# Compressed keys and values one job later, selection rounds after the gate's turned part

## What is computed

```
h   = rms_norm(x) * (1 + scale) + shift            # scale, shift, gate = silu(c) @ w_ada + b_ada
f   = h @ w_in                                     # columns shared out among both mixers
ck  = silu(flat(cmp_k rows + pe) @ w1[0]) @ w2[0]  # compressed keys,   31 per prompt head, 15 per sample
cv  = silu(flat(cmp_v rows + pe) @ w1[1]) @ w2[1]  # compressed values
o_n = g0*attend(q, ck, cv) + g1*attend(selected blocks) + g2*attend(window)
o_d = attend over the top-k keys by the indexer's score   (k = 128 for the prompt, 65 for samples)
y   = x + gate * ((sig(m_n) * up(o_n*silu(z_n)) + sig(m_d) * up(o_d*silu(z_d))) @ w_out)
```

## Time and profile before

| | |
|---|---|
| median of 3 runs (lowest, highest) | 618.58 us (617.23, 623.91) |
| the profiled execution: time, span | 616.9 us, 615.1 us |
| mean granted clock of TensorE | 0.993 |
| PE busy | 585.8 us, 95% of the span |
| DVE busy | 337.8 us, 55% |
| ACT busy | 247.6 us, 40% |
| POOL busy | 151.4 us, 25% |
| DMA | 68.37 MB, mean 111 GB/s |

### The profile page before, as it was taken

How to read it: one execution, slowest core, us unless ns; L and a number is a source line. 1 busy time by engine, 2 the same in 40 slices (tenths; PEclk the granted TensorE clock), 3 DMA queues, 4 the chain that set the end, 5 groups by cost and what they waited for, 6 DMA issues and landing times.

```text
span 615.1 us, 12161 instructions
## 1 busy us (share of the span) xinstructions
PE 585.8 (95%) x4630; PEld 481.0 (78%) x4630; DVE 337.8 (55%) x847; ACT 247.6 (40%) x549; POOL 151.4 (25%) x196
## 2 busy tenths in 40 slices
PE   4999999998999999989999999999999999999995
PEld 1487776765776887766766769999999999998784
DVE  0454025968978556878766654442322633227873
ACT  6232245143131345656567545343222232223443
POOL 1226350360350445643644430000000000000130
PEclk9899999999899999999999999999999999999999
DMA  9991731421452264001301207229332242434003
GB/s 305 385 343 26 289 128 39 143 67 52 131 156 73 71 174 139 2 1 44 95 3 52 87 4 189 84 69 267 119 69 76 87 113 69 100 108 137 1 30 117
DMA packets 52426, 68.37 MB, mean 111 GB/s; under 512 B 5089, under 2 KB 34969, under 8 KB 52208
## 3 DMA queue, kind: packets, MB, share of 16 engines
q1 hardware_dynamic: 49744, 56.85, 30.4%
q10 hardware_dynamic: 1808, 6.31, 3.0%
q0 software_dynamic: 816, 4.43, 1.8%
HBM read 62.99 MB, written 6.66 MB: 113 GB/s over the span
## 4 chain that ended last, share of the span: by engine, by line
PE 85%; DVE 9%; issue 3%; ACT 2%; DMA 1%; POOL 0%; SPq 0%; DVEq 0%; ACTq 0%
PE psum L1162 29%; PE psum L935 8%; PE psum L937 7%; PE psum L936 7%; PE psum L1424 5%; PE psum L1392 4%; PE psum L1347 4%; PE psum L1262 3%; PE psum L1069 2%; PE psum L961 2%; DVE psum L2080 2%; PE psum L950 1%; DVE score L2004 1%; DVE top L2003 1%; DVE rT L1999 1%
## 5 line engine op out<-in xcount | busy, mean ns | idle before, releaser
L1552 ACT ACTIVATE w_hi<-stage 128x1024 fp32r<-128x1024 f32 (+2 forms) x56 | 56.1, 1002 | 159.8 <-PE psum L1162 94.0
L1894 DVE TENSOR_TENSOR w_lo<-stage,w_hi 128x1024 fp32r<-128x1024 f32 x34 | 41.7, 1225 | 111.2 <-ACT w_hi L1552 108.0
L1162 PE MATMUL psum<-hT_hi,w_hi 128*128 128x272 f32 x368 | 76.4, 289 | 0.6 <-DVE w_lo L1894 0.6
L1162 PE MATMUL psum<-hT_lo,w_hi 128*128 128x272 f32 x368 | 76.2, 288 | 0.0
L1162 PE MATMUL psum<-hT_hi,w_lo 128*128 128x272 f32 x368 | 75.9, 288 | 0.0
L845 POOL TENSOR_TENSOR w_lo<-stage,w_hi 128x1024 fp32r<-128x1024 f32 (+2 forms) x22 | 44.2, 2008 | 107.9 <-ACT w_hi L1552 107.9
L935 PE MATMUL psum<-w_hi,hT_hi 128*128 128x512 f32 (+3 forms) x192 | 69.4, 361 | 0.7 <-issue 0.5
L936 PE MATMUL psum<-w_hi,hT_lo 128*128 128x512 f32 (+3 forms) x192 | 66.8, 348 | 0.0
L937 PE MATMUL psum<-w_lo,hT_hi 128*128 128x512 f32 (+3 forms) x192 | 66.7, 347 | 0.0
L926 POOL TENSOR_TENSOR y<-y,final_g 128x512 f32<-128x512 f32 (+1 forms) x5 | 7.8, 1588 | 217.2 <-ACT merged L1782 217.2
L1162 PEld LDWEIGHTS psum<-hT_hi,w_hi 128*128 128x128 f32 x368 | 57.8, 188 | 1.1 <-DVE w_lo L1894 1.1
(11 more groups left out here) (346 smaller groups left out, 1122.0 us busy)
## 6 DMA issues: line engine op xcount, KB each, us to landing
stage<-in_w_in SPq DMA_DIRECT2D x14, 1024.0 KB, 5.3
stage<-in_w_ada SPq DMA_DIRECT2D x8, 1024.0 KB, 10.2
stage<-in_w_in SPq DMA_DIRECT2D x10, 512.0 KB, 5.3
staging<-in_x_prompt ACTq DMA_DIRECT2D x4, 512.0 KB, 5.7
cached<-in_cache_nsa_kv SPq DMA_DIRECT2D x32, 64.0 KB, 2.3
stage<-in_cache_nsa_kv SPq DMA_DIRECT2D x16, 128.0 KB, 2.1
stage<-in_state_nsa_win_kv SPq DMA_DIRECT2D x2, 1024.0 KB, 7.2
stage<-in_cache_dsa_kv SPq DMA_DIRECT2D x16, 128.0 KB, 2.1
```

The costliest lines, as they stand in the source:

```text
L1162: last = mm(out[:, h, :], left[w][:, k, P * x:P * x + P], halves(mov[m])[:, h, :], start=(k == 0 and w + m == 0), stop=(k == tiles - 1 and ...
L1552: last = A(dst, src, ACT.Copy)
L1894: last = tt(dst, src, hi.bitcast(F32), ALU.subtract)
```

## The change

In the list of small work "ck" moves from slot 3, between "mod" and "modT" of part (4, 1), to the front of slot 4. "cvp" and the two "cvs" move from slot 4, between "mod" and "modT" of part (5, 0), to the front of slot 5. In VectorE's list the eight rounds that stood ahead of the wait for "ck" now stand behind the copy of "modT" (4, 1); the four and four rounds that stood ahead of the wait for "cvp" now stand behind the copy of "modT" (5, 0). No instruction is added or taken away. The rounds are those of `take_top`: one `max` and one `match_replace`.

```diff
     queries(3, ROT, range(2, 4))
-    for kind, n, e in (("qs", ROT, "v"), ("hid", 0, "a"), ("mod", (4, 1), "a"), ("ck", 0, "v"), ("modT", (4, 1), "v")):
+    for kind, n, e in (("qs", ROT, "v"), ("hid", 0, "a"), ("mod", (4, 1), "a"), ("modT", (4, 1), "v")):
         add(3, kind, n, e)
+
+    add(4, "ck", 0, "v")
     queries(4, DSAQ, range(2))
...
-    for kind, n, e in (("qs", DSAQ, "v"), ("hid", 1, "a"), ("mod", (5, 0), "a"), ("cvp", 0, "v"), ("cvs", 0, "a"),
-                       ("cvs", 1, "v"), ("modT", (5, 0), "v")):
+    for kind, n, e in (("qs", DSAQ, "v"), ("hid", 1, "a"), ("mod", (5, 0), "a"), ("modT", (5, 0), "v")):
         add(4, kind, n, e)
-    for kind, n, e in (("mod", (5, 1), "a"), ("selx", 0, "a"), ("selx", 1, "a"), ("modT", (5, 1), "v"),
+    for kind, n, e in (("cvp", 0, "v"), ("cvs", 0, "a"), ("cvs", 1, "v"), ("mod", (5, 1), "a"), ("selx", 0, "a"), ("selx", 1, "a"), ("modT", (5, 1), "v"),
                        ("grow", 0, "v"), ("grow", 1, "v"), ("k", WIN, "a"), ("kn", WIN, "v")):
         add(5, kind, n, e)
...
                             tt(dst, dst, part_t, ALU.add).then_inc(*tell(aux_dve))
+                        if n == (4, 1):
+                            rounds(2, 8)
+                        elif n == (5, 0):
+                            rounds(2, 4)
+                            rounds(3, 4)
                         continue
-                    if kind == "ck":
-                        rounds(2, 8)
-                    elif kind == "cvp":
-                        rounds(2, 4)
-                        rounds(3, 4)
                     dve.wait_ge(aux_done, i + 1)
```

## The result

The changed kernel takes 636.86 us (median of 6 runs, 636.45 to 642.14) against 619.22 us for the kernel before (617.23 to 623.91): ratio 1.0292, 95% interval 1.0251 to 1.0333. It is slower, as forecast; the forecast was 638, range 631.5 to 643. The profiled execution took 636.45 us with a span of 634.6, 19.5 more than the span of before. Two spans of one execution each differ by other things too: in this one "hid" of slot 3 begins at 142.31 instead of 141.73, a difference that arises ahead of everything the change touches. So I count every milestone from the start of that "hid".

The account below looks back on a forecast made before the run. The prediction took PE to bound the kernel (85% of the chain of waits, busy 95% of the span). Its terms, 10.0 + 5.9 + 1.9 + 1.7 = 19.5 us onto 616.9, gave 636.4, as a median 638, range 631.5 to 643.

Parts of the forecast that it names:

- PE, slot 3: "ck" leaves slot 3, but "modT" still waits for ScalarE's copy of "mod": gain 0, PE's idle time 1.9 us.
- PE, slot 4: "ck" at the front is covered by the queries' wait: cost 0; "modT" at the end comes 1.0 us earlier.
- VectorE, job 3: Eight rounds behind "modT" delay job 3's reads, so PE ends job 4's first piece late: cost 10.0 us.
- VectorE, job 4: Four and four rounds behind "modT" delay job 4's reads beyond VectorE's idle time, PE waits: cost 5.9 us.
- PE, slot 5: "cvp" and "cvs" arrive ahead of "mod" with nothing to cover them: cost 1.9 us.
- clock: PE's granted clock falls after each long stall: cost 0 after the first, 1.7 us after the second.
- The 1.1 us that the prediction worked out for that case: Added to the sum if PE returned from both stalls at 1.2 GHz, the throttled clock.
- The 1.7 us added for the median: The kernel before's median, 618.58, lay 1.7 above its profiled execution; added to 636.4 to forecast the median, 638.
- C: Rival: only half the delay reaches PE because VectorE regains time; 13.1 us, so 631.7; chance 0.10.
- D: Rival: VectorE's room takes the moved rounds in full; -0.8 us, so 617.8, no difference; chance 0.04.
- A: Rival: the clock stays full after the stalls; 17.8 us more, so 636.4; chance 0.18.
- B: Rival: longer clock falls, "ck" uncovered, slot 4's turning and copying begun at half clock; 23.3 us, so 642; chance 0.15.

Follow-up runs that it names:

- e1: The changed kernel with VectorE's rounds of both slots put back under "hid", ahead of the wait for "modT": 623.31 us against 619.23, ratio 1.005.
- e4: The changed kernel with only the eight rounds of slot 3 put back under "hid": 629.1 us against 621.99, ratio 1.0121.
- e2: The kernel before with only VectorE's rounds moved behind the copy of "modT", no matmuls moved: 637.95 us against 619.23, ratio 1.0278.
- e3: The changed kernel with only the four and four rounds of slot 4 put back under "hid": 631.1 us against 619.22, ratio 1.0163.
- e8: The kernel before with four of slot 3's eight rounds moved behind the copy of "modT": 623.65 us against 621.99, ratio 1.004.
- e7: The changed kernel with unread extra matmuls, 24 ahead of job 4's sample tile and 30 ahead of job 5's: 640.24 us against 621.99, ratio 1.0302.
- e5: The kernel before with "ck" and "modT" (4, 1) at the head of slot 4, the eight rounds still under "hid": ratio 0.9955.
- e9: A repetition of e5, the same kernel measured again: ratio 0.9997.
- e6: As e5, but the four rounds of tile 2 ahead of job 3's reads are shared out to jobs 4 and 5: ratio 0.9994.
- e10: A repetition of e6, the same kernel measured again: ratio 0.9974.

## Why the prediction was right, point by point

- **PE, slot 3: 0.** Right. "modT" starts 12.18 us after "hid" in both traces, and the wait ahead of it is 1.90 us, as said.
- **PE, slot 4.** "ck" under cover: 0 forecast, 0.3 measured where nothing else delays the piece (e1 and e4, queries 37.48 after "hid" against 37.22). The prediction read the start of the last tile as 177.7. It is 177.89, so PE's path from VectorE's last read to the queries is 1.8 us (e1, e4) and not 1.5:

```profile
177.89 0.29 PE L935 MATMUL psum<-w_hi,hT_hi 128*128 128x280 f32 x1
```

The earlier "modT" shows: 0.87 us of wait, then its matmuls; it is spent in the second stall, as forecast, and comes out only where that stall is gone (e1, -0.6 at job 5's sample tile).
- **VectorE, job 3: 10.0 forecast, 9.0 measured.** The mechanism was right, the size off by one instruction. The mask that ends the samples' selection took 1.45 us in the kernel before and 0.30 here (last section), so 1.15 of the 10.0 came back. The first read started 24.84 us after the first late round instead of 25.98. e2 and e3 repeat the delay, 8.9 and 9.3, without and with the moved matmuls; e8 halves the rounds and gets 3.85. For the same reason the first stall is 6.24 us and not 7.3.
- **VectorE, job 4: 5.9 forecast, 6.3 measured** (15.28 - 9.01). e4 has it alone: 6.3.
- **PE, slot 5: 1.9, and clock: 1.7.** Together 3.6 measured (18.91 - 15.28). Of these 1.7 is the slower first piece of job 5 (5.94 us instead of 4.24), and 1.9 the moved steps. The clock falls inside each stall, at about 179.3 and 223.7, and is still at 0.50 when PE comes back:

```profile
179.00:180.00 1.00, 0.00 (x0) 0.65 0.75 203
...
181.00:182.00 1.00, 0.64 (x13) 0.50 0.00 0
...
223.00:224.00 1.00, 0.00 (x0) 0.84 0.00 0
```

The fall after the first stall cost nothing, as forecast (e7, 46.22 against 46.23). By the Trainium skill (TensorE: Matmul & The Clock Gate, "What's actually happening") the throttled state is the default: the trace agrees, the clock is 0.50 at both returns. The 1.1 us that the prediction worked out for that case did not come, since the reads set PE's pace there. The prediction's side remark of four matmuls a us in a fall against five to six behind it is a misreading: the count takes in every matmul that touches the window. From start to start they are 0.43 us apart in the fall at 156 (156.40, 156.82) and 0.23 behind it (159.23, 159.46).
- **Sum:** 9.0 + 6.3 + 1.9 + 1.7 = 18.9, forecast 19.5. The medians differ by 17.6. Some of the nearness is luck. The terms of the two VectorE stages were off by -1.0 and +0.4, and the profiled execution meets the 636.4 (636.45) only because its "hid" began 0.6 us later. The 1.7 us added for the median did not come either: the median of the changed kernel is 0.4 above its profiled execution.
- **Rivals.** C (half of the delay absorbed) and D (all of it) fell: e8 shows that even four rounds find no room, since the reads' pace passes the delay on tile by tile, and to the queries through GpSimd's adds. A (the clock stays full after the stalls) gave 636.4, which is nearer to the measured 636.86 than the forecast of 638, but its mechanism is refuted by the trace: the clock was 0.50 at both returns. B's longer falls with "ck" uncovered are not in this trace; e3 has such a one (clock 0.54 at 186 to 188, queries 9.3 us late instead of 9.0). The medians alone could not tell the forecast from A or B, since executions of the changed kernel go from 636.45 to 642.14. Of the chances, the forecast, A, B and C add up to 0.96, not 0.95.

## What to carry to other kernels

An instruction moved past a wait in an in-order list moves everything behind that wait too: ask first what the engine did while it waited. Here 21 us of selection were free only because they stood ahead of the wait, and moved behind it they cost about 15, three quarters of it. And judge the room ahead of a chain of per-tile reads at its last tile, not at its first: 2.8 us at the sample tile were 0.45 at the last one (read until 177.44, used from 177.89), and none at the queries, which start 0.15 us after the GpSimd add that follows the last read.

## What the runs showed of the hardware that I had not expected

**A VectorE instruction that takes 0.30 or 1.45 us.** The selection's mask (a TENSOR_SCALAR of 32 x 288) in the kernel before, and the GpSimd instruction that ran at the time:

```profile
164.56 1.45 DVE L2013 TENSOR_SCALAR score_sample<-score_sample 32x288 f32<-32x288 f32 x1
```

```profile
163.44 2.41 POOL L845 TENSOR_TENSOR w_lo<-stage,w_hi 128x1024 fp32r<-128x1024 f32 x1 [3.70 <-ACT w_hi L1552]
```

The mask ends at 166.01, GpSimd's instruction at 165.85. In e1 and e4, where it starts beside the same GpSimd work, it takes 1.44 and 1.40; in the other nine profiles, the changed kernel's among them, it starts outside it and takes 0.30. The two instructions of a round beside the same GpSimd work keep their 0.45 and 0.43 us. By the Trainium skill (SBUF — State Buffer, "Who interferes with whom") VectorE and GpSimd share a port pair, whoever is first holds it for its whole instruction, and a `tensor_scalar` is of the kind that can ask for it; the traces agree in that VectorE's instruction ends 0.16 us after GpSimd's; the ports themselves no run shows. I had priced 25.98 us of VectorE work as one block and not looked for such a row in it.

**The same kernel with and without a fall of the clock.** e5 and e9 are one kernel. In slot 5, at the same place of the same list, first e5, then e9:

```profile
218.00:220.00 2.00, 2.00 (x10) 0.53 1.05 380
220.00:222.00 2.00, 2.00 (x13) 0.62 1.11 340
```

```profile
218.00:220.00 2.00, 2.00 (x16) 1.00 1.04 378
220.00:222.00 2.00, 2.00 (x20) 1.00 1.14 332
```

From "hid" to the end of job 5 it is 88.62 in one and 87.26 in the other: 1.4 us for the fall. Such falls stand in or right behind stretches of small matmuls in e1, e2, e3, e4, e5, e7 and e8, and not at those places in the kernel before, the changed kernel, e6, e9 and e10. In slot 5 of e1 PE was busy without a gap for the six us ahead of the fall (216 to 222). A single profile therefore can't price an effect under two us by its end; milestones counted from a common point can, as long as no fall lies between them. What decides in which execution the fall comes stays open.
